# Head turns at half-chunk 21, six output turns one block earlier, and the delta chain respaced, in a two-stage float32 block on one core

## Chip, cores and metric

The kernel runs on one NeuronCore of a Trainium2 chip. The metric is the device time of one execution in microseconds; the profile shows one execution of the same program, instruction by instruction.

## What is computed

Two stages over 256 tokens of width 2048, all in float32. The first holds a gated delta rule with 16 heads, a convolution branch and two gated products; the second holds two layers with memory attention, pooling or block attention, and an output product. The parts that the change touches are these:

```python
qkv = jax.nn.silu(causal_depthwise_conv(qkv, w_conv_qkv[i]))      # per head: q, k, v
o_a = gated_delta_chunked(q, k, v, g_log, beta)                   # 16 heads, chunks of 64
...
mixed = jnp.concatenate([branch * jax.nn.silu(gate_b), mem_o * jax.nn.silu(gate_m)], axis=-1)
y = mixed @ w_out[i]                                              # i = 0, 1
h = layer_norm(DEEPNORM_ALPHA * h + y, ln_g[i], ln_b[i])
```

## The kernel before

**Blocks and half-chunks.** All large products are one long row of blocks. A block is 256 tokens by 512 weight columns, contracted over 2048 channels: 16 chunks of 128 channels, each for two tiles of 128 tokens. A chunk for one tile is a half-chunk (`hs`, 0 to 31 in a block). In each, PE runs three matmuls into a `pair` bank (L460 to L462): the weights are split into a high and a low part (`w_hi`, `w_lo`), and so are the activations (`in_hi`, `in_lo`). The splits are made beside it: ACT copies a raw weight chunk to `w_hi` (L434), DVE subtracts it to `w_lo` (L441), both up to six chunks ahead of PE; `w_hi` and `w_lo` hold eight chunks, so that ACT waits on `chunk_used`, which PE raises after each chunk. SP loads the raw weights.

**Work beside the blocks.** Everything else is hung into the same half-chunks of the four engines by hand: each `..._pe`, `..._act`, `..._dve` function is called with `hs` after PE's three matmuls of that half-chunk, after ACT's piece at even `hs`, and before DVE's piece at odd `hs`. The numbers in `if hs == ...` are therefore the order on each engine, and semaphores connect the engines. All engines run their own list in order.

**Head blocks (0 to 15, their beside work one block later).** Per head: PE turns the projected q, k, v to channel columns at `hs` 3 (L514), DVE and ACT make the four-tap convolution (L544, L607), ACT takes the tanh at 14 (L548), DVE the silu at 16 (L616, `silu_done`), PE turns the result to tokens (L520) and multiplies keys by keys and queries (L525) at 19, ACT copies the tokens to `tok` at 20 (L555) and sums squares at 21 (L564), POOL makes scales of them (L580 to L591), and DVE uses those at `hs` 1 of the next block (L638). The loops over heads run two heads a pass.

**Delta blocks (the four blocks from `BLK_GB`, one group g of four heads each).** A chain passes from PE to ACT or DVE and back through the banks RA, RB and QA: x (PE 2, DVE 3), d (PE 5, DVE 6: `tt`, L899), then for each 128-token tile y (L787), z (L795), v (L800), its copy `vn` on DVE (L907), and the output products. The tile-0 steps stand at 7 to 16 and the tile-1 steps at 17 to 26, where DVE's sum of squares (L925) is the last; POOL turns it into `orn` (L885, L887), and in the next block DVE scales `o_t` with it at `hs` 4 (L934), PE turns that to columns at 8 (L835), ACT and DVE split it (L870, L945). SP waits for steps of this chain before it loads the next group's tiles; the last such load (`tt`, L723) waits for `v_done1`.

**Output blocks (`BLK_OUT0`, `BLK_OUT1`, four blocks each).** Their activations are the gated columns `mo`, turned by PE two channel chunks at a time (a pair or turn g, 0 to 7, four transposes, L1108), copied to `in_hi` by ACT (L1115) and to `in_lo` by DVE (L1121, `turned_lo`). They overwrite the `in_hi`, `in_lo` that the input blocks before still read. Turn 0 stands ahead of the first output block, turns 1 to 7 at its half-chunks 0, 3, 7, 11, 15, 19, 23. The gating of columns 512·n is done by ACT and DVE at `hs` 2 and 5 of the block behind the gate's product (L1680, L1691, L1703, `mixed_ready`); the fourth such one lies in the first output block.

Of the kernel before, what the change touches and what calls it, by code (L numbers as in the profile page):

```python
# [112 lines left out]
def program(nc, t, out, ctx):  # L113
# [393 lines left out]
    def keys_pe(pe, h, hs):  # L507
        if hs == 3:
            pe.wait_ge(psum_free, BLK_A + h + 1)
            reach(pe, s["tok_ready"], h)  # L510
            for c in range(3):
                bank = QB[:, 0:S] if c == 2 else QA[:, c * S:(c + 1) * S]
                for tile in range(TT):
                    mm = pe.transpose(bank[:, tile * P:(tile + 1) * P], proj[:, tile, c * P:(c + 1) * P], ident)  # L514
            mm.then_inc(s["qkv_cols"], 1)
        if hs == 19:
            pe.wait_ge(s["silu_done"], h + 1)
            for tile in range(TT):
                for c in range(3):
                    mm = pe.transpose((QA, QB)[tile][:, c * P:(c + 1) * P], conv[:, c, tile * P:(tile + 1) * P], ident)  # L520
            mm.then_inc(s["qkv_tokens"], 1)
            reach(pe, s["ap_ready"], h)
            for tile in range(TT):
                own = slice(tile * P, (tile + 1) * P)
                mm = pe.matmul(RA[:, tile * S:(tile + 1) * S], conv[:, 1, own], conv[:, 0:2, own], start=True, stop=True)  # L525
            mm.then_inc(s["kk_done"], 1)

    def keys_act(act, h, par, hs):
# [17 lines left out]
        if hs == 14:  # L546
            act.wait_ge(tap_done, SHORT * h + SHORT)
            act.activation(conv_th[:, :, :], conv[:, :, :], ACT.Tanh, scale=0.5).then_inc(s["conv_tanh"], 1)  # L548
        if hs == 20:
            act.wait_ge(s["qkv_tokens"], h + 1)  # L550
            act.wait_ge(s["silu_done"], h + 1)
            act.dma_start(ex_dram[GROUP * (h % GROUP) + h // GROUP, :, EX_KQ:EX_END].rearrange("p (c n) -> p c n", c=2),
                          conv[:, 0:2, P:S]).then_inc(s["kq_stored"], 16)
            reach(act, s["tok_scaled"], h)
            act.activation(tok[:, 0].rearrange("p c n -> p (c n)"), QA[:, 0:3 * P], ACT.Copy)  # L555
            act.activation(tok[:, 1].rearrange("p c n -> p (c n)"), QB[:, 0:3 * P], ACT.Copy)\
               .then_inc(s["tok_ready"], 1)
        if hs == 21:
            act.wait_ge(s["tok_ready"], h + 1)
            reach(act, s["scal_ready"], h)  # L560
            for tile in range(TT):
                for c in range(2):
                    n = 2 * tile + c
                    act.activation(junk[:, n], tok[:, tile, c], ACT.Square, accum_out=ssq[:, n:n + 1])\  # L564
                       .then_inc(s["norms_summed"], 1)
# [195 lines left out]
    def rule_pe(pe, g, hs):  # L761
# [10 lines left out]
        if hs == 5:  # L772
            reach(pe, s["tt_zeroed"], 2 * g)
            for tile in range(TT):
# [3 lines left out]
                mm.then_inc(s["rule_on_pe"], 1)  # L778
        for tile, at in ((0, 7), (1, 17)):
            if hs == at:  # L780
# [16 lines left out]
            if hs == at + 4:  # L797
# [3 lines left out]
                mm.then_inc(s["rule_on_pe"], 1)  # L801
        if hs == 13:
            pe.wait_ge(*step("v_ready0", g))
# [8 lines left out]
            mm.then_inc(s["rule_on_pe"], 1)  # L812
        if hs == 15:
            pe.wait_ge(*step("s1_ready", g))
# [5 lines left out]
            mm.then_inc(s["rule_on_pe"], 1)  # L820
        if hs == 23:
            pe.wait_ge(*step("v_ready1", g))
# [15 lines left out]
    def rule_act(act, g, hs):  # L838
        for tile, at in ((0, 8), (1, 18)):
            if hs == at:  # L840
# [7 lines left out]
        if hs == 14:  # L848
# [3 lines left out]
        if hs == 16:  # L852
            act.wait_ge(*step("qs1_done", g))
# [3 lines left out]
            ins.then_inc(s["rule_on_act"], 1)  # L857
        if hs == 25:
            act.wait_ge(*step("o_ready1", g))
# [29 lines left out]
    def rule_dve(dve, g, hs):  # L889
# [10 lines left out]
        for tile, at in ((0, 12), (1, 22)):  # L900
            if hs == at:
# [5 lines left out]
                dve.tensor_copy(vn[:, :, :], four_of(RA)).then_inc(s["rule_on_dve"], 1)  # L907
        if hs == 14:
# [3 lines left out]
        if hs == 16:  # L912
            dve.wait_ge(*step("ks1_done", g))
# [3 lines left out]
            ins.then_inc(s["rule_on_dve"], 1)  # L917
        if hs == 24:
            dve.wait_ge(*step("o_done1", g))
            dve.wait_ge(*step("oq_ready", g))  # L920
            dve.tensor_tensor(o_t[:, 1], four_of(RB), oq[:, :, :], ALU.add).then_inc(s["rule_on_dve"], 1)
        if hs == 26:
            dve.wait_ge(*step("o_squared", g))
# [831 lines left out]

    OWN_AT = {0: 1, 3: 2, 7: 3, 11: 4, 15: 5, 19: 6, 23: 7}

# [16 lines left out]
    def beside_pe(pe, blk, hs):  # L1774
# [34 lines left out]
        if blk in OWN and hs in OWN_AT:  # L1809
            own_pe(pe, blk, OWN_AT[hs])  # L1810
        if blk in OWN and hs % 4 == 3 and hs < 28:
            pe.wait_ge(s["turned_lo"], OWN[blk][0] + (hs + 1) // 4 + 1)
        pool_pe(pe, blk, hs)
        attention(at, lambda i, h, second: attend_pe(pe, i, h, second))

    def before_pe(pe, blk):
# [17 lines left out]
        if blk in OWN:  # L1834
            own_pe(pe, blk, 0)
            pe.wait_ge(s["turned_lo"], OWN[blk][0] + 1)

# [15 lines left out]
    def beside_act(act, blk, hs):  # L1853
# [94 lines left out]

    def before_act(act, blk):
        if blk in OWN:  # L1950
            own_act(act, blk, 0)

    def tail_act(act):
        for blk in range(BLK_GB, BLK_END):
            before_act(act, blk)
            act_block(act, blk, lambda hs: beside_act(act, blk, hs))
# [5 lines left out]
    def beside_dve(dve, blk, hs):  # L1962
# [457 lines left out]
```

## Time and profile before

| | us |
|---|---|
| median of three runs | 2133.61 (2132.96 to 2133.75) |
| profiled execution | 2134.15 |
| its span, first to last instruction | 2132.1 |
| PE busy | 2100.2 (99%) |
| DVE, ACT, POOL busy | 1474.3 (69%), 1228.0 (58%), 334.6 (16%) |

PE is busy nearly all the time, at a granted clock of 0.998 of full speed. Ends of PE's instructions are modelled, so an idle time of PE in a row is only part of what a wait costs: the distances between starts tell the whole. A regular matmul of a block starts 0.23 us behind the one before it, so that a half-chunk of three takes 0.68 us.

### The profile page before, as it was taken

How to read it: one execution, taken by the hardware profiler on the slowest of the kernel's cores; microseconds unless marked ns; L12 is line 12 of the kernel's file. 1: busy time of each engine (PE TensorE's matmuls, PEld its weight loads, DVE VectorE, ACT ScalarE, POOL GpSimd, SP SyncE). 2: the span in 40 equal slices, each digit the busy share in tenths (PEclk: the TensorE clock that was granted, in tenths of full speed). 3: DMA queues.
4: the chain of work that ended last, by engine and by line, in shares of the span. 5: the costliest groups of instructions: out<-in, count | busy, mean ns of one | idle time of the engine just before them, and what ended most of it. 6: DMA issues, size and time to landing. Idle time of an engine off the chain costs nothing.

```text
span 2132.1 us, 28652 instructions
## 1 busy us (share of the span) xinstructions
PE 2100.2 (99%) x9841; PEld 1733.5 (81%) x9841; DVE 1474.3 (69%) x2676; ACT 1228.0 (58%) x2359; POOL 334.6 (16%) x468
## 2 busy tenths in 40 slices
PE   7999999999999999999999999999999999999998
PEld 6888888888888888888888877887888888888886
DVE  6777777788999977569665655643666745456666
ACT  6666666677777764457555544543554555555543
POOL 1111111156665641010000000000000000000000
PEclk9999999999999999999999999999999999999999
DMA  8777766789877866576777665655665555644462
GB/s 248 231 210 207 201 196 192 202 223 266 228 208 211 233 209 212 191 263 210 260 265 251 224 209 168 212 178 163 233 221 197 182 180 195 197 158 139 158 217 99
DMA packets 434689, 439.68 MB, mean 206 GB/s; under 512 B 27728, under 2 KB 306384, under 8 KB 432144
## 3 DMA queue, kind: packets, MB, share of 16 engines
q1 hardware_dynamic: 412752, 381.76, 58.1%
q0 software_dynamic: 7600, 35.79, 5.0%
q10 hardware_dynamic: 14224, 20.71, 2.7%
q8 instruction: 61, 1.00, 0.2%
q14 instruction: 52, 0.43, 0.1%
HBM read 410.92 MB, written 27.28 MB: 206 GB/s over the span
## 4 chain that ended last, share of the span: by engine, by line
PE 81%; DVE 14%; issue 2%; ACT 2%; DMA 0%; POOL 0%; DVEq 0%; SPq 0%; POOLq 0%; ACTq 0%
PE pair L460 24%; PE pair L462 24%; PE pair L461 24%; DVE w_lo L441 5%; DVE conv L607 2%; DVE QB L1058 2%; ACT conv L544 1%; PE QA L1489 1%; PE RA L1505 1%; PE RA L525 1%; DVE conv L616 1%; DVE ap L659 1%; DMA raw<-in_w_in_dram 0%; PE QB L1574 0%; PE QA L520 0%
## 5 line engine op out<-in xcount | busy, mean ns | idle before, releaser
L441 DVE TENSOR_TENSOR w_lo<-raw,w_hi 128x512 fp32r<-128x512 f32 x1368 | 920.8, 692 | 401.1 <-ACT w_hi L434 399.2
L434 ACT ACTIVATE w_hi<-raw 128x512 fp32r<-128x512 f32 x1368 | 826.9, 625 | 450.4 <-PE pair L462 445.0
L460 PE MATMUL pair<-w_hi,in_hi 128*128 128x512 f32 x2336 | 932.9, 399 | 3.9 <-DVE in_lo L1121 2.8
L462 PE MATMUL pair<-w_hi,in_lo 128*128 128x512 f32 x2336 | 911.1, 390 | 0.0
L461 PE MATMUL pair<-w_lo,in_hi 128*128 128x512 f32 x2336 | 909.8, 389 | 0.0
L462 PEld LDWEIGHTS pair<-w_hi,in_lo 128*128 128x128 f32 x2336 | 438.4, 188 | 93.4
L460 PEld LDWEIGHTS pair<-w_hi,in_hi 128*128 128x128 f32 x2336 | 439.0, 188 | 92.5 <-DVE in_lo L1121 3.3
L461 PEld LDWEIGHTS pair<-w_lo,in_hi 128*128 128x128 f32 x2336 | 439.2, 188 | 87.9 <-issue 1.0
L1027 POOL TENSOR_TENSOR acc_p<-acc_p,tap 128x256 f32<-128x256 f32 x160 | 184.2, 1151 | 38.7 <-ACT tap L1001 25.3
L1001 ACT ACTIVATE tap<-upad,cwl 128x256 f32<-128x256 f32 x192 | 96.7, 507 | 51.9 <-POOL acc_p L1027 50.9
L1058 DVE SCALAR_TENSOR_TENSOR QB<-upad,cwl,QB 128x256 f32<-128x256 f32 x272 | 119.5, 478 | 0.0
L607 DVE SCALAR_TENSOR_TENSOR conv<-conv_in,cw,conv 128x256 f32<-128x256 f32 x144 | 61.1, 479 | 7.4 <-ACT conv L544 7.4
L2106 POOL DMA_DIRECT2D ln_vec_a<-in_ln_g_dram x1 | 0.5, 531 | 350.7 <-DVE mo L1703 350.7
L580 POOL TENSOR_TENSOR an<-ssq,pool_eps 128x4 f32<-128x4 f32 x16 | 3.2, 201 | 333.5 <-ACT junk L564 333.5
L460 PE MATMUL pair<-w_hi,mem_hi 128*128 128x512 f32 x128 | 51.9, 406 | 0.0
L460 PE MATMUL pair<-w_hi,oa_hi 128*128 128x512 f32 x128 | 50.9, 398 | 0.0
L460 PE MATMUL pair<-w_hi,ub_hi 128*128 128x512 f32 x128 | 50.2, 392 | 0.0
L462 PE MATMUL pair<-w_hi,mem_lo 128*128 128x512 f32 x128 | 50.1, 391 | 0.0
L461 PE MATMUL pair<-w_lo,mem_hi 128*128 128x512 f32 x128 | 50.0, 390 | 0.0
L462 PE MATMUL pair<-w_hi,oa_lo 128*128 128x512 f32 x128 | 49.9, 390 | 0.0
L461 PE MATMUL pair<-w_lo,oa_hi 128*128 128x512 f32 x128 | 49.9, 390 | 0.0
L462 PE MATMUL pair<-w_hi,ub_lo 128*128 128x512 f32 x128 | 49.9, 390 | 0.0
(394 smaller groups left out, 1806.8 us busy)
## 6 DMA issues: line engine op xcount, KB each, us to landing
raw<-in_w_in_dram SPq DMA_DIRECT2D x512, 256.0 KB, 4.0
raw<-in_w_in_dram SPq DMA_DIRECT2D x80, 1024.0 KB, 5.2
raw<-in_w_out_dram SPq DMA_DIRECT2D x48, 1024.0 KB, 5.0
raw<-in_w_kv_shared_dram SPq DMA_DIRECT2D x24, 1024.0 KB, 5.1
raw<-in_w_br_a_dram SPq DMA_DIRECT2D x16, 1024.0 KB, 6.4
raw<-in_w_br_b_dram SPq DMA_DIRECT2D x16, 1024.0 KB, 6.8
raw<-in_w_mem_kv_dram SPq DMA_DIRECT2D x16, 1024.0 KB, 5.0
raw<-in_w_ple_gate_dram SPq DMA_DIRECT2D x16, 1024.0 KB, 5.0
```

The costliest lines, as they stand in the source:

```text
L434: act.activation(piece(blk, q)[0], raw[:, u, q % UK], ACT.Copy).then_inc(hi_ready[u], 1)
L441: dve.tensor_tensor(lo, raw[:, u, q % UK], hi.bitcast(F32), ALU.subtract).then_inc(lo_ready[u], 1)
L460: pe.matmul(o, xh, wh, start=(q == 0), stop=False)
L461: pe.matmul(o, xh, wl, start=False, stop=False)
L462: mm = pe.matmul(o, xl, wh, start=False, stop=(q == KC - 1))
L525: mm = pe.matmul(RA[:, tile * S:(tile + 1) * S], conv[:, 1, own], conv[:, 0:2, own], start=True, stop=True)
L544: ins = act.activation(conv[:, c], conv_in[:, c, 0:S], ACT.Copy, scale=cw[:, 0, c:c + 1])
L607: ins = dve.scalar_tensor_tensor(conv[:, c], conv_in[:, c, k:k + S], cw[:, k, c:c + 1], conv[:, c], ALU.mult, ALU.add)
L616: dve.scalar_tensor_tensor(conv[:, :, :], conv_th[:, :, :], 1.0, conv[:, :, :], ALU.add, ALU.mult)\
L1001: act.activation(tap[:, n % 2], upad[:, par, k:k + S], ACT.Copy, scale=cwl[:, k:k + 1])\
L1027: pool.tensor_tensor(acc_p[:, :], tap[:, 0] if n == 1 else acc_p[:, :], tap[:, n % 2], ALU.add)\
L1058: dve.scalar_tensor_tensor(a, src, cwl[:, k:k + 1], a, ALU.mult, ALU.add).then_inc(long_tap[k % 2], 1)
```

## The change

No instruction is added and none is taken away; places in the order move. Three parts:

- Heads: PE's turn to tokens goes from `hs` 19 to 21, with it ACT's copy from 20 to 22 and its squares from 21 to 23.
- Delta chain: tile 0's y, z, v from 7, 9, 11 to 8, 10, 12, `vn` from 12 to 13, the products behind it from 13 and 15 to 15 and 17, tile 1's from 17, 19, 21 to 20, 22, 24, `vn` from 22 to 25, the rest from 23 to 26 to 26 to 30.
- Output turns: 0 to 5 go to half-chunks 12, 14, 17, 20, 24, 28 of the last input block, where ACT waits for the old columns to have been used (`chunk_used`); 6 and 7 stand at 8 and 10 of the first output block. PE waits once for six `turned_lo` ahead of that block, and for all eight at its `hs` 23.

```diff
 def keys_pe(pe, h, hs):
-        if hs == 19:
+        if hs == 21:
             pe.wait_ge(s["silu_done"], h + 1)
...
 def rule_pe(pe, g, hs):
-        for tile, at in ((0, 7), (1, 17)):
+        for tile, at in ((0, 8), (1, 20)):
             if hs == at:
                 pe.wait_ge(*step("t64_ready1", g))
...
-        if hs == 13:
+        if hs == 15:
             pe.wait_ge(*step("v_ready0", g))
...
 def rule_dve(dve, g, hs):
-        if hs == 26:
+        if hs == 30:
             dve.wait_ge(*step("o_squared", g))
...
-    OWN_AT = {0: 1, 3: 2, 7: 3, 11: 4, 15: 5, 19: 6, 23: 7}
+    OWN_AHEAD = {12: 0, 14: 1, 17: 2, 20: 3, 24: 4, 28: 5}
+    OWN_AT = {8: 6, 10: 7}
...
+    def own_ahead_pe(pe, blk, g):
+        if g == 0:
+            heads = MEM_HEADS if blk == BLK_OUT0 else len(ATTEND)
+            pe.wait_ge(s["att_ready"], heads)
+            pe.wait_ge(s["probT_ready"], heads)
+            pe.wait_ge(s["scores_masked"], heads)
+        own_pe(pe, blk, g)
+
+    def own_ahead_act(act, blk, g):
+        act.wait_ge(chunk_used, (KC - 1) * (blk - 1) + 2 * g + 2)
+        own_act(act, blk, g)
...
-        if blk in OWN and hs % 4 == 3 and hs < 28:
-            pe.wait_ge(s["turned_lo"], OWN[blk][0] + (hs + 1) // 4 + 1)
+        if blk in OWN and hs == 23:
+            pe.wait_ge(s["turned_lo"], OWN[blk][0] + 8)
+        if blk + 1 in OWN and hs in OWN_AHEAD:
+            own_ahead_pe(pe, blk + 1, OWN_AHEAD[hs])
...
         if blk in OWN:
-            own_pe(pe, blk, 0)
-            pe.wait_ge(s["turned_lo"], OWN[blk][0] + 1)
+            pe.wait_ge(s["turned_lo"], OWN[blk][0] + 6)
```

PE in a head block, at the turn to tokens (`silu_done` is DVE's silu, `lo_ready2` a chunk of `w_lo`):

```order
 L461 MATMUL pair<-w_lo,in_hi 128x512
 L462 MATMUL pair<-w_hi,in_lo 128x512
+L460 MATMUL pair<-w_hi,in_hi 128x512 [waits lo_ready2]
+L461 MATMUL pair<-w_lo,in_hi 128x512
+L462 MATMUL pair<-w_hi,in_lo 128x512
+L460 MATMUL pair<-w_hi,in_hi 128x512
+L461 MATMUL pair<-w_lo,in_hi 128x512
+L462 MATMUL pair<-w_hi,in_lo 128x512
 L520 MATMUL QA<-const,conv 128x128 [waits silu_done]
 L520 MATMUL QA<-const,conv 128x128 x2
```

Two half-chunks of the block's own matmuls now stand ahead of the waiting transposes.

PE at the start of the first output block, before:

```order
L462 MATMUL pair<-w_hi,in_lo 128x512
L1108 MATMUL QA<-const,mo 128x128 [waits turned_lo,mixed_ready]
L1108 MATMUL QA<-const,mo 128x128 x3
L460 MATMUL pair<-w_hi,in_hi 128x512 [waits lo_ready0,psum_free,turned_lo]
L461 MATMUL pair<-w_lo,in_hi 128x512
L462 MATMUL pair<-w_hi,in_lo 128x512
L1108 MATMUL QB<-const,mo 128x128 [waits turned_lo,mixed_ready]
L1108 MATMUL QB<-const,mo 128x128 x3
```

and in the changed program, from the last turn of the input block on (`turned_lo` is DVE's low part of the turned columns):

```order
L1108 MATMUL QB<-const,mo 128x128 [waits turned_lo,mixed_ready]
L1108 MATMUL QB<-const,mo 128x128 x3
L460 MATMUL pair<-w_hi,in_hi 128x512
L461 MATMUL pair<-w_lo,in_hi 128x512
L462 MATMUL pair<-w_hi,in_lo 128x512
L460 MATMUL pair<-w_hi,in_hi 128x512 [waits lo_ready3]
L461 MATMUL pair<-w_lo,in_hi 128x512
L462 MATMUL pair<-w_hi,in_lo 128x512
L460 MATMUL pair<-w_hi,in_hi 128x512
L461 MATMUL pair<-w_lo,in_hi 128x512
L462 MATMUL pair<-w_hi,in_lo 128x512
L460 MATMUL pair<-w_hi,in_hi 128x512 [waits lo_ready0,psum_free,turned_lo]
```

Turn 0 stood between the blocks and was waited for at once; now nothing stands between them, and the wait for `turned_lo` has three half-chunks behind turn 5.

PE in the second delta block, half-chunks 6 to 8, before (`rule_on_dve` is the chain's `tt`, `og_ready` DVE's scaled `o_t`):

```order
L460 MATMUL pair<-w_hi,in_hi 128x512
L461 MATMUL pair<-w_lo,in_hi 128x512
L462 MATMUL pair<-w_hi,in_lo 128x512
L787 MATMUL RA<-vbk_113,tt_112 128x128 [waits vbk_loaded,rule_on_dve]
L787 MATMUL RA<-vbk_113,tt_112 128x128 x3
L460 MATMUL pair<-w_hi,in_hi 128x512 [waits lo_ready1]
L461 MATMUL pair<-w_lo,in_hi 128x512
L462 MATMUL pair<-w_hi,in_lo 128x512
L835 MATMUL QA<-const,o_t 128x128 [waits u_ready,og_ready]
L835 MATMUL QA<-const,o_t 128x128 x3
L835 MATMUL QB<-const,o_t 128x128 x4
```

and in the changed program, from the same half-chunk on:

```order
L460 MATMUL pair<-w_hi,in_hi 128x512
L461 MATMUL pair<-w_lo,in_hi 128x512
L462 MATMUL pair<-w_hi,in_lo 128x512
L460 MATMUL pair<-w_hi,in_hi 128x512 [waits lo_ready1]
L461 MATMUL pair<-w_lo,in_hi 128x512
L462 MATMUL pair<-w_hi,in_lo 128x512
L787 MATMUL RA<-vbk_113,tt_112 128x128 [waits vbk_loaded,rule_on_dve]
L787 MATMUL RA<-vbk_113,tt_112 128x128 x3
L835 MATMUL QA<-const,o_t 128x128 [waits u_ready,og_ready]
L835 MATMUL QA<-const,o_t 128x128 x3
L835 MATMUL QB<-const,o_t 128x128 x4
```

The chain's step L787 goes behind one more half-chunk and stands directly ahead of the turns L835. On ACT, in the same block, the split of those turned columns (L870) stood behind the chain's copy L847 and now stands ahead of it.

## Rows read from the trace of the kernel before

**Rows 1.** The page, busy time of each engine.
```profile
PE 2100.2 (99%) x9841; PEld 1733.5 (81%) x9841; DVE 1474.3 (69%) x2676; ACT 1228.0 (58%) x2359; POOL 334.6 (16%) x468
```
**Rows 2.** Waits of PE, PEld, ACT: line <- releaser: us in total, times, longest.
```profile
PE QA L520 <- DVE conv L616: 3.5, 15, 0.2
PE pair L460 <- DVE in_lo L1121: 2.8, 2, 1.4
...
PEld QA L520 <- DVE conv L616: 9.9, 15, 0.7
...
PEld RA L787 <- DVE tt L899: 2.0, 3, 1.1
...
PEld RB L805 <- DVE vn L907: 1.8, 3, 0.7
...
ACT w_hi L434 <- PE pair L462: 445.0, 603, 4.6
```
**Rows 3.** Timeline of PE at a head's turn: start us, us, instruction [idle <-releaser].
```profile
228.81 0.39 PE L462 MATMUL pair<-w_hi,in_lo 128*128 128x512 f32 x1
229.43 0.55 PE L520 MATMUL QA<-const,conv 128*128 128x128 f32 x3 [0.23 <-DVE conv L616]
229.81 0.49 PE L520 MATMUL QB<-const,conv 128*128 128x128 f32 x3
```
**Rows 4.** Timeline of PE at a turn of the same block that doesn't wait.
```profile
217.24 0.39 PE L462 MATMUL pair<-w_hi,in_lo 128*128 128x512 f32 x1
217.47 0.60 PE L514 MATMUL QA<-const,proj 128*128 128x128 f32 x4
217.91 0.38 PE L514 MATMUL QB<-const,proj 128*128 128x128 f32 x2
```
**Rows 5.** Timeline of DVE in the same head, from the first tap to the silu.
```profile
220.72 1.28 DVE L607 SCALAR_TENSOR_TENSOR conv<-conv_in,cw,conv 128x256 f32<-128x256 f32 x3 [0.44 <-ACT conv L544]
...
228.42 0.95 DVE L616 SCALAR_TENSOR_TENSOR conv<-conv_th,conv 128x768 f32<-128x768 f32 x1
```
**Rows 6.** Timelines of ACT, POOL and DVE from a head's turn into the next block.
```profile
215.53 0.68 ACT L534 ACTIVATE proj<-pair,small 128x512 f32<-128x512 f32 x1
...
211.25 0.19 POOL L591 TENSOR_TENSOR scal<-scal,hst 128x2 f32<-128x2 f32 x1
...
213.50 0.48 DVE L638 TENSOR_SCALAR ex<-tok,scal 128x128 f32<-128x128 f32 x2
```
**Rows 7.** Timeline of PE at the start of the first output block.
```profile
1569.08 0.60 PE L1108 MATMUL QA<-const,mo 128*128 128x128 f32 x4
1571.09 0.50 PE L460 MATMUL pair<-w_hi,in_hi 128*128 128x512 f32 x1 [1.41 <-DVE in_lo L1121]
...
1571.89 0.60 PE L1108 MATMUL QB<-const,mo 128*128 128x128 f32 x4
1572.25 0.48 PE L460 MATMUL pair<-w_hi,in_hi 128*128 128x512 f32 x1
```
**Rows 8.** Timelines of PE and DVE at the start of the last input block.
```profile
1547.31 0.39 PE L460 MATMUL pair<-w_hi,in_hi 128*128 128x512 f32 x1
...
1550.54 1.23 DVE L1703 TENSOR_TENSOR mo<-mo,stage 128x1024 f32<-128x1024 f32 x1
```
**Rows 9.** Timelines of PE and DVE in the second delta block, the waiting step.
```profile
814.74 0.40 PE L462 MATMUL pair<-w_hi,in_lo 128*128 128x512 f32 x1
815.77 1.16 PE L787 MATMUL RA<-vbk,tt 128*128 128x128 f32 x8 [0.64 <-DVE tt L899]
...
815.03 0.68 DVE L899 TENSOR_TENSOR tt<-RB,tt 128x512 f32<-128x512 f32 x1
```
**Rows 10.** SP's `tt` loads there, landing of all loads of L723, PE's next need.
```profile
835.96 2.15 SPq L723 DMA_DIRECT2D tt<-inverse_blocks  x4
...
DMA to landing us min/median/max: 2.0/4.2/9.8
...
845.53 1.05 PE L770 MATMUL RA<-t,ap 128*128 128x128 f32 x8
```

More of the change, by code:

```diff
@@ L548, in keys_act @@
             act.activation(conv_th[:, :, :], conv[:, :, :], ACT.Tanh, scale=0.5).then_inc(s["conv_tanh"], 1)
-        if hs == 20:
+        if hs == 22:
             act.wait_ge(s["qkv_tokens"], h + 1)
@@ L557, in keys_act @@
                .then_inc(s["tok_ready"], 1)
-        if hs == 21:
+        if hs == 23:
             act.wait_ge(s["tok_ready"], h + 1)
@@ L812, in rule_pe @@
             mm.then_inc(s["rule_on_pe"], 1)
-        if hs == 15:
+        if hs == 17:
             pe.wait_ge(*step("s1_ready", g))
@@ L820, in rule_pe @@
             mm.then_inc(s["rule_on_pe"], 1)
-        if hs == 23:
+        if hs == 26:
             pe.wait_ge(*step("v_ready1", g))
@@ L838, in rule_act @@
     def rule_act(act, g, hs):
-        for tile, at in ((0, 8), (1, 18)):
+        for tile, at in ((0, 9), (1, 21)):
             if hs == at:
@@ L847, in rule_act @@
                 act.activation(zneg[64:P].rearrange("p h n -> p (h n)"), RB[64:P, :], ACT.Copy, scale=-1.0).then_inc(s["rule_on_act"], 1)
-        if hs == 14:
+        if hs == 16:
             act.wait_ge(*step("s1_done", g))
@@ L851, in rule_act @@
             act.activation(s1[:, :, :].rearrange("p h n -> p (h n)"), RB[:, :], ACT.Copy).then_inc(s["rule_on_act"], 1)
-        if hs == 16:
+        if hs == 18:
             act.wait_ge(*step("qs1_done", g))
@@ L857, in rule_act @@
             ins.then_inc(s["rule_on_act"], 1)
-        if hs == 25:
+        if hs == 28:
             act.wait_ge(*step("o_ready1", g))
@@ L899, in rule_dve @@
                 dve.tensor_tensor(tt4[:, tile], four_of((RA, RB)[tile]), tt4[:, tile], ALU.add).then_inc(s["rule_on_dve"], 1)
-        for tile, at in ((0, 12), (1, 22)):
+        for tile, at in ((0, 13), (1, 25)):
             if hs == at:
@@ L907, in rule_dve @@
                 dve.tensor_copy(vn[:, :, :], four_of(RA)).then_inc(s["rule_on_dve"], 1)
-        if hs == 14:
+        if hs == 16:
             dve.wait_ge(*step("o_done0", g))
@@ L911, in rule_dve @@
             dve.tensor_copy(o_t[:, 0], four_of(QA)).then_inc(s["rule_on_dve"], 1)
-        if hs == 16:
+        if hs == 18:
             dve.wait_ge(*step("ks1_done", g))
@@ L917, in rule_dve @@
             ins.then_inc(s["rule_on_dve"], 1)
-        if hs == 24:
+        if hs == 27:
             dve.wait_ge(*step("o_done1", g))
@@ L1930, in beside_act @@
             own_act(act, blk, OWN_AT[hs])
+        if blk + 1 in OWN and hs in OWN_AHEAD:
+            own_ahead_act(act, blk + 1, OWN_AHEAD[hs])
         attention(at, lambda i, h, second: attend_act(act, i, h, second))
@@ L2040, in beside_dve @@
             own_dve(dve, blk, OWN_AT[hs])
+        if blk + 1 in OWN and hs in OWN_AHEAD:
+            own_dve(dve, blk + 1, OWN_AHEAD[hs])
         if hs == 0 and (BLK_OUT0 <= done < BLK_OUT0 + 3 or BLK_OUT1 <= done):
@@ L2061, in ple_dve @@
                .then_inc(s["mo_scaled"], 1)
-    def before_dve(dve, blk):
-        if blk in OWN:
-            own_dve(dve, blk, 0)
     def tail_dve(dve):
         for blk in range(BLK_GB, BLK_END):
-            before_dve(dve, blk)
             dve_block(dve, blk, lambda hs: beside_dve(dve, blk, hs))
```

4 lines of the change are left out of this document (removed).

## Prediction

> **What bounds the kernel.** I read the page first: PE is busy for 99% of the span, DVE for 69%, ACT for 58% [rows 1]. So PE's own list sets the time, and since the change adds and removes no instruction, only PE's waits can pay. The list of waits shows which there are [rows 2]: fifteen waits of the heads' turn L520 for DVE's silu, two of an output block's first matmul for `in_lo`, and, best seen on PE's weight loads (PEld), three of the chain's L787 for `tt` and three of L805 for `vn`. Idle time is only a part of what such a wait costs, so I then took timelines of PE around one wait of each kind and measured from start to start.
>
> **Heads' turns, hs 19 to 21.** Ahead of L520 the last matmul starts at 228.81 and the first transpose at 229.43: 0.62 us [rows 3]. The turn L514, which waits for nothing, starts 0.23 us behind its matmul [rows 4]. That is 0.39 us lost. The three transposes after the wait take 0.38 us (229.43 to 229.81), where four without one take 0.44 (217.47 to 217.91), so three 0.33: 0.05 more. 0.44 us a head, 15 heads: **6.6 us**.
>
> Would the wait be gone? DVE ends the silu at 229.37 [rows 5], just ahead of PE's 229.43. Two half-chunks of three matmuls at 0.23 us bring PE there 1.36 us later than it could before, and the wait was 0.39, so PE comes 0.97 us after the silu. The silu doesn't move with it: nothing from the first tap on waits for the turn, and the pieces of ACT and DVE in between are held by PE's chunks as before.
>
> What is late instead: ACT's copy and squares, POOL's scales, and DVE's use of them at hs 1 of the next block. POOL ends at 211.44, DVE starts at 213.50 [rows 6]: 2.06 us to spare. The turn comes 0.92 us later in its block (1.36 less 0.44) and the next block begins 0.44 us sooner, so 0.70 us are left. ACT's drain of the next product ends at 216.21 [rows 6], 1.26 us ahead of the turn L514 at 217.47 [rows 4] that reads it. The DMA of old queries and keys that ACT issues at hs 20 moves with the copy to 22; `conv` is written again only at hs 5 of the next block. I take nothing for these.
>
> **Output turns.** The first turn starts at 1569.08 and the block's first matmul at 1571.09, 2.01 us, where a turn inside the block takes 0.36 (1571.89 to 1572.25) [rows 7]. The difference, 1.65 us, is lost ahead of each of the two output blocks: the waits of rows 2 are two, with 1.4 us of idle each. **3.3 us.** The eight turns themselves cost PE the same in any block. Two new places to wait:
> - Turn 5 is at hs 28 and the output block waits for its `turned_lo`. From its start PE has 0.36 us of transposes and three half-chunks, 2.04 us, together 2.40, and 2.01 are needed [rows 7]. 0.4 us to spare; at worst, one more 128x512 step of DVE in the way (0.68 us as in rows 9), 0.3 us a block.
> - Turn 6 moves from hs 19 to hs 8 of the output block and needs the fourth gating. One block earlier the third gating ends at 1551.77, 4.46 us behind that block's first matmul at 1547.31 [rows 8]. PE reaches its turn at hs 8 after nine half-chunks, 6.1 us. 1.6 us to spare, as ACT and DVE no longer begin the block with turns.
>
> In the input block ACT and DVE get six turns, in a block where ACT waits for PE's chunks anyway (0.74 us a time, rows 2), and the attention that shares the banks has ended. Nothing.
>
> **Delta chain.** At its worst place the last matmul starts at 814.74 and L787 at 815.77 [rows 9]: 1.03 us against 0.23, 0.80 lost and a little for the restart. For all six I scale from the heads, where PEld's idle is 9.9/15 = 0.66 us for a loss of 0.44, the idle less 0.22. L787: 2.0 - 3 x 0.22 = 1.3 us; L805: 1.8 - 0.66 = 1.1; 2.4 together [rows 2]. One half-chunk more (0.68 us) ahead of L787 covers the two shorter waits (0.9 us of PEld idle for both) and all but 0.1 of the long one: PE arrives at 815.65 for a `tt` that DVE ends at 815.71 [rows 9]. L805 gets a half-chunk more behind the step that feeds `vn`. I take **2.3**, and 1.0 as the lower end, if DVE, busy without a break ahead of `tt` there, slips with PE.
>
> What is late instead: the last sum of squares goes from hs 26 to 30, and DVE's use of POOL's result stays at hs 4 of the next block. SP's loads of `tt`, which wait for PE's step `v`, go back by three half-chunks, 2.04 us. They are issued from 835.96 to 838.11, land 4.2 us after issue in the median, and PE needs them at 845.53 [rows 10]: 838.11 + 2.04 + 4.2 = 844.35, 1.2 us to spare. The weight load behind them in SP's queue waits for DVE's piece at hs 27 and so isn't held up. Nothing.
>
> **Sum.** 6.6 + 3.3 + 2.3 = 12.2 us. Against the profiled execution of 2134.15 (span 2132.1 and 2.05 around it) that is 2121.95; the median of the runs lies 0.54 lower than that execution, so **2121.4 us**, 0.57% faster. The three terms stand one after the other on PE's list, so they add.
>
> **Two rules of a page.** The Trainium skill ("Perfetto Trace Analysis", Tensor Engine Instruction) says that the end of a PE instruction in a profile is an estimate, while its start is observed. The trace agrees: 128x512 matmuls listed at 0.39 us start 0.23 apart. By it the idle rows understate a wait, which speaks for the start distances and against the third rival.
> The same page (Identifying Performance Opportunities, "Consistent bubbles") says that one gap repeated over a stretch can mean too little buffer space. By that rule fifteen equal gaps would not go away with a later place; the first rival is that case.
>
> **Rivals.**
> - The heads' wait comes back: the silu depends on space that PE frees, and is as late at hs 21 as at 19. Then 12.2 - 6.6 = 5.6 us remain: 2128.0. For it: the gap is the same in every head. Against it: DVE is busy from 220.72 to 229.37 and started on ACT's first tap [rows 5], which hangs on PE's hs 3 at 217.47 [rows 4]. That chain has a fixed length of 11.9 us, and PE's way gets 1.36 us longer.
> - The output blocks wait again, at turn 5 or at the gating for turn 6: up to 3.3 us given back, 2124.7. The 0.4 or the 1.6 us above would have to be used up.
> - The rest of each start distance is no wait and stays. Then PE's idle counts: 3.5 + 2.8, and for the chain 3.8 of PEld's idle by the heads' ratio 3.5/9.9, 1.3: 7.6 us in all, 2126.0. Against it: L514 has the same neighbours and not that distance [rows 4].
> - **Slower**: ACT's copy and squares, 0.92 us later in a block that ends 0.44 sooner, push ACT's drain past the turn L514 that reads it. The margin is 1.26 [rows 4, 6], the shift 1.36, so even with no recovery PE waits 0.1 us. If ACT also loses a piece and its wait for PE (0.74 us, rows 2), or more, PE waits w in each of 16 heads: 2121.4 + 16 w. From w = 0.77 us that is slower than before, and w = 1.1 gives 2139.0. Against it: ACT has such a wait for PE at nearly each chunk, and makes up for the shift in two of them.
> - The `tt` loads land late. With 9.8 us, the longest in rows 10, PE waits 4.4 us in each of three blocks, 13 us, and nothing is left: 2134.6.
>
> **Chances and range.** Forecast 0.78; heads' wait back 0.08; output blocks 0.04; idle rows 0.04; `tt` late 0.03; slower 0.03. The forecast's own range is 2119.8 (restart costs of 0.1 us at the chain's six places, and 1 us between runs) to 2123.3 (chain 1.0, 0.3 at each output block). With the output and idle cases beside it, 2119.8 to 2126.0 leaves 0.14 out, and holds 8 in 10 with some error of my own. A measurement here can tell 0.2%, 4.3 us, from no change. Below 2129.3 are all cases but the last two: faster 0.93, no change 0.04, slower 0.03.
>
> **What would show it.** In the profile after: no wait of L520 for L616, and 0.23 us from matmul to L520 in every head; no wait of L460 for L1121, and 0.23 us across the start of both output blocks; L787 and L805 with one short wait at most. The prediction is wrong if a wait of PE for DVE, ACT or a DMA is new at L514, L770, L1108 or at the new place of L520.

## The result, and the profile after

The changed kernel takes 2120.56 us in the median of four runs (2119.98 to 2120.67), beside 2133.40 (2132.96 to 2133.75) of the kernel before measured on the same chip. The ratio is 0.9937, with a 95% interval of 0.9926 to 0.9949: 12.84 us less, where 12.2 us were forecast (the forecast time was 2121.4 us). The profiled execution took 2119.98, its span 2118.2.

The page of after, busy time of each engine, answers to [rows 1]: PE has the same 9841 instructions.

```profile
PE 2094.6 (99%) x9841; PEld 1735.4 (82%) x9841; DVE 1472.7 (70%) x2676; ACT 1226.7 (58%) x2359; POOL 336.3 (16%) x468
```

PE's whole list of waits after (line <- releaser: us in total, times, longest) answers to [rows 2].

```profile
PE pair L1197 <- DVE in_lo L1137: 10.9, 1, 10.9
PE QA L971 <- DVE z2b L1040: 0.7, 3, 0.3
PE QA L1108 <- DVE xr L1615: 0.6, 1, 0.6
PE QB L1369 <- DVE sqb L1418: 0.4, 1, 0.4
PE QA L1226 <- DVE sgl L1321: 0.3, 1, 0.3
PE pair L460 <- DVE w_lo L441: 0.3, 1, 0.3
PE QA L1223 <- DVE sgl L1316: 0.2, 1, 0.2
```

The lines of L520, of L460 for L1121, of L787 and of L805 are gone, on PE and on PEld, and no line is new. What is left is in stages that the change doesn't touch; the longest, L1197, is PE's first instruction, which starts 10.9 us into the program.

A head's turn after, in timelines of PE (start us, us, instruction), DVE, and PE at the turn L514 of the same block, answers to [rows 3 to 5].

```profile
226.74 0.39 PE L462 MATMUL pair<-w_hi,in_lo 128*128 128x512 f32 x1
226.97 0.49 PE L520 MATMUL QA<-const,conv 128*128 128x128 f32 x3
227.30 0.49 PE L520 MATMUL QB<-const,conv 128*128 128x128 f32 x3
...
225.00 0.95 DVE L616 SCALAR_TENSOR_TENSOR conv<-conv_th,conv 128x768 f32<-128x768 f32 x1
...
214.05 0.60 PE L514 MATMUL QA<-const,proj 128*128 128x128 f32 x4
```

L520 now starts 0.23 us behind its matmul, not 0.62, and three transposes take 0.33, not 0.38. The silu ends at 225.95, 1.02 us ahead of L520, and 11.90 us behind this block's L514 (214.05), as before (217.47 to 229.37).

The start of the first output block after, PE and DVE, answers to [rows 7] and, for the fourth gating, to [rows 8].

```profile
1558.85 0.60 PE L1108 MATMUL QB<-const,mo 128*128 128x128 f32 x4
1559.20 0.48 PE L460 MATMUL pair<-w_hi,in_hi 128*128 128x512 f32 x1
...
1561.14 0.40 PE L462 MATMUL pair<-w_hi,in_lo 128*128 128x512 f32 x1
1561.37 0.39 PE L460 MATMUL pair<-w_hi,in_hi 128*128 128x512 f32 x1
...
1567.50 0.60 PE L1108 MATMUL RA<-const,mo 128*128 128x128 f32 x4
...
1560.17 0.69 DVE L1121 SCALAR_TENSOR_TENSOR in_lo<-QB,in_hi 128x512 fp32r<-128x512 f32 x1 [1.30 <-ACT in_hi L1115]
...
1564.60 1.23 DVE L1703 TENSOR_TENSOR mo<-mo,stage 128x1024 f32<-128x1024 f32 x1
```

The output block begins at 1561.37, 0.23 us behind the matmul before it. Turn 5 (1558.85) has its last piece at 1560.86, 0.51 us ahead. The gating ends at 1565.83, turn 6 starts at 1567.50.

The second delta block after, PE and DVE, answers to [rows 9]; here PE starts L787 0.22 us behind its matmul and L805 0.23.

```profile
807.88 0.39 PE L462 MATMUL pair<-w_hi,in_lo 128*128 128x512 f32 x1
808.10 1.05 PE L787 MATMUL RA<-vbk,tt 128*128 128x128 f32 x8
...
807.05 0.68 DVE L899 TENSOR_TENSOR tt<-RB,tt 128x512 f32<-128x512 f32 x1
...
816.23 0.39 PE L462 MATMUL pair<-w_hi,in_lo 128*128 128x512 f32 x1
816.46 0.72 PE L805 MATMUL RB<-vn,vbk 128*128 128x128 f32 x5
```

**The sum from both traces.** With the start distances of every place, each less the undisturbed 0.23 us (or 0.11 between transposes), the kernel before loses 5.91 + 0.86 = 6.77 us at L520, 3.31 at the two output blocks, and 1.55 + 1.35 = 2.90 at L787 and L805. That is 12.98 us, and 0 at all of them after. The median fell by 12.84. The spans of the two profiled executions differ by 13.9 us, and 0.8 of that lies ahead of the first head's turn L514, at a wait at the program's start (L460 for `w_lo`, 1.1 us before and 0.3 after), which differs from execution to execution and which the change doesn't touch (last section).

### The profile page after: what moved, and what is told of

Its sections match the earlier page's. It is cut to its first block, busy times and chain, and to the rows that moved or that the text cites. A ratio compares the mean times of both kernels' runs of the same rounds, so it can differ in the third digit from the quotient of the medians.

```text
span 2118.2 us, 28654 instructions
## 1 busy us (share of the span) xinstructions
PE 2094.6 (99%) x9841; PEld 1735.4 (82%) x9841; DVE 1472.7 (70%) x2676; ACT 1226.7 (58%) x2359; POOL 336.3 (16%) x468
## 4 chain that ended last, share of the span: by engine, by line
PE 89%; DVE 8%; issue 1%; ACT 1%; DMA 1%; POOL 1%; DVEq 0%; ACTq 0%; POOLq 0%
PE pair L460 26%; PE pair L462 26%; PE pair L461 26%; DVE w_lo L441 3%; DVE QB L1058 2%; PE QA L1489 1%; PE RA L1505 1%; PE RA L525 1%; POOL acc_p L1027 0%; PE QB L1574 0%; PE RA L1731 0%; PE RB L1731 0%; DMA x_cols<-in_x_columns_dram 0%; PE pair L481 0%; PE pair L482 0%
## 5 line engine op out<-in xcount | busy, mean ns | idle before, releaser
L441 DVE TENSOR_TENSOR w_lo<-raw,w_hi 128x512 fp32r<-128x512 f32 x1368 | 919.6, 693 | 392.9 <-ACT w_hi L434 391.0
L460 PE MATMUL pair<-w_hi,in_hi 128*128 128x512 f32 x2336 | 932.8, 399 | 0.3 <-DVE w_lo L441 0.3
L460 PEld LDWEIGHTS pair<-w_hi,in_hi 128*128 128x128 f32 x2336 | 439.0, 188 | 88.5 <-DVE w_lo L441 1.1
L460 PE MATMUL pair<-w_hi,mem_hi 128*128 128x512 f32 x128 | 51.9, 406 | 0.0
L460 PE MATMUL pair<-w_hi,oa_hi 128*128 128x512 f32 x128 | 50.9, 398 | 0.0
L460 PE MATMUL pair<-w_hi,ub_hi 128*128 128x512 f32 x128 | 50.2, 392 | 0.0
```

The lines of the kernel that those rows point to most:

```text
L441: dve.tensor_tensor(lo, raw[:, u, q % UK], hi.bitcast(F32), ALU.subtract).then_inc(lo_ready[u], 1)
L460: pe.matmul(o, xh, wh, start=(q == 0), stop=False)
```

## Experiments

The kernels ran in three sets, each on a chip of its own with the kernel before beside it: 2133.93 us in the first, 2133.69 in the second and 2133.74 in the third. Gains in the medians are taken against the kernel before of the same set. Intervals of ratios are of 95%, against the kernel before.

### The three parts, each alone

Heads alone (`heads_only`), on the kernel before:

```diff
-        if hs == 19:
+        if hs == 21:
             pe.wait_ge(s["silu_done"], h + 1)
...
-        if hs == 20:
+        if hs == 22:
             act.wait_ge(s["qkv_tokens"], h + 1)
...
-        if hs == 21:
+        if hs == 23:
             act.wait_ge(s["tok_ready"], h + 1)
```

> The kernel before with the heads' turns alone moved (19 to 21, and their two ACT steps by two). Theory of the prediction: what a wait costs is the distance from the end of the turn's last matmul before it to the start of L520, here 0.44 us in each of 15 heads, so 6.6 us less than before, about 2126.8. Rival: only the idle time that the PE rows name is worth something (some 0.23 us a head), so 3.5 us less, about 2130. Second rival: the span follows the longest engine and not the wait, so nothing.

Measured: 2127.28 us (2126.98 to 2128.53), ratio 0.9970 (0.9959 to 0.9981): 6.65 us less. The rival of idle rows (2130) falls, and so does that of no gain.

Output turns alone (`own_only`), the core of the edit:

```diff
-    OWN_AT = {0: 1, 3: 2, 7: 3, 11: 4, 15: 5, 19: 6, 23: 7}
+    OWN_AHEAD = {12: 0, 14: 1, 17: 2, 20: 3, 24: 4, 28: 5}
+    OWN_AT = {8: 6, 10: 7}
...
-            own_pe(pe, blk, 0)
-            pe.wait_ge(s["turned_lo"], OWN[blk][0] + 1)
+            pe.wait_ge(s["turned_lo"], OWN[blk][0] + 6)
```

> The kernel before with the six gated pairs turned in the block ahead, and the last two at half-chunks 8 and 10 of the output block. Theory: 1.65 us in each of the two output blocks, 3.3 us less than before, about 2130.1. Rival by idle rows alone: 2.8 less. Rival that the turns in the input block cost PE time of their own: less than 3.3 by about 0.3 us for each block.

Measured: 2130.25 us (2129.45 to 2131.80), ratio 0.9984 (0.9975 to 0.9993): 3.68 us less, for 3.3 expected. Its trace shows that the turns cost nothing more in the input block: each starts 0.23 or 0.24 us behind its matmul and takes 0.35 or 0.36, as inside an output block before. Between 3.3 and the idle rows' 2.8 the median alone doesn't decide, since the interval holds both; the starts (3.31) are what speaks for the first.

The chain alone (`chain_only`), the core of the edit:

```diff
-        for tile, at in ((0, 7), (1, 17)):
+        for tile, at in ((0, 8), (1, 20)):
...
-        if hs == 13:
+        if hs == 15:
             pe.wait_ge(*step("v_ready0", g))
...
-        for tile, at in ((0, 12), (1, 22)):
+        for tile, at in ((0, 13), (1, 25)):
             if hs == at:
                 dve.wait_ge(*step(f"v_done{tile}", g))
```

> The kernel before with the delta chain's steps alone at half-chunks 8 to 30. Theory: the waits of L787 and L805 go, whose start distances beyond an undisturbed step add up to 2.9 us, of which the prediction took 2.3 and kept 0.1 as left over; about 2130.8. Rival by idle rows: 1.3 less, about 2132.1. If this alone gives nothing, the three parts don't add up and the gain of the whole sits elsewhere.

Measured: 2130.51 us (2130.30 to 2131.59), ratio 0.9986 (0.9977 to 0.9995): 3.42 us less. Its trace has no wait of L787 or L805. The idle rows' 1.3 us falls (it would give 2132.6); the start distances' 2.9 stands, 0.5 below what was measured. The three gains add up to 13.75 us, where the whole gave 12.84, 0.9 less. All three are taken against the same median of the kernel before, so that an error in it counts three times, and that median differs by up to 0.5 us between the sets (2133.40 to 2133.93). So the parts add to within 1 us, and these medians can't show more; by the starts in the traces the three terms add to 12.98.

### What the wait at L520 is made of

Here L520 is put nearer and further away in the kernel after. (Where the expectation says "ACT's silu", the silu is DVE's, L616.) First `heads18`:

```diff
-        if hs == 21:
+        if hs == 18:
             pe.wait_ge(s["silu_done"], h + 1)
...
-        if hs == 22:
+        if hs == 20:
             act.wait_ge(s["qkv_tokens"], h + 1)
...
-        if hs == 23:
+        if hs == 21:
             act.wait_ge(s["tok_ready"], h + 1)
```

> The kernel after with the heads' turns on PE at half-chunk 18 and ACT's steps at 20 and 21. Theory of the prediction (ACT's silu ends at a time fixed by the head's earlier steps, so PE loses every step by which it comes sooner): at 19 PE lost 0.44 us, at 18 it comes 0.68 us earlier and loses 1.12 us, in 15 heads 16.8 us more than the kernel after, about 2137.4. Rival (the loss is a fixed hand-over between PE and ACT wherever the turn stands): 0.44 us a head, about 2127.2.

Measured: 2137.66 us (2137.18 to 2138.38), ratio 1.0019 (1.0009 to 1.0029), against 2137.4 by the theory and 2127.2 by the rival. The kernel is slower than before. Its timelines of PE and DVE at the same head:

```profile
231.75 0.39 PE L462 MATMUL pair<-w_hi,in_lo 128*128 128x512 f32 x1
233.07 0.55 PE L520 MATMUL QA<-const,conv 128*128 128x128 f32 x3 [0.93 <-DVE conv L616]
233.46 0.49 PE L520 MATMUL QB<-const,conv 128*128 128x128 f32 x3
...
232.07 0.95 DVE L616 SCALAR_TENSOR_TENSOR conv<-conv_th,conv 128x768 f32<-128x768 f32 x1
```

PE starts L520 1.32 us behind its matmul, 1.09 more than undisturbed, and loses 0.06 among the transposes: 1.15 us a head, 17.2 in fifteen. The median rose by 17.1. The row itself says 0.93. At 19 the loss was 0.44, so one half-chunk (0.68 us) costs 0.71: the silu ends 11.91 us behind L514 (221.11 to 233.02), the same time as before, and PE pays each step by which it is early.

`heads20` has 20, 21, 22 in the same three places.

> The kernel after with the heads' turns at 20, ACT's steps at 21 and 22. Theory: silu ends 1.02 us ahead of L520 at 21, so 0.34 us ahead at 20: no wait, same as the kernel after within 0.2 us, about 2120.6. Rival (a fixed hand-over, which 21 escapes by an accident of order): 0.44 us a head, about 2127.2.

Measured: 2120.38 us (2120.22 to 2122.24), ratio 0.9940 (0.9923 to 0.9957). No wait of L520. PE and DVE at the same head:

```profile
226.16 0.39 PE L462 MATMUL pair<-w_hi,in_lo 128*128 128x512 f32 x1
226.38 0.49 PE L520 MATMUL QA<-const,conv 128*128 128x128 f32 x3
...
225.10 0.94 DVE L616 SCALAR_TENSOR_TENSOR conv<-conv_th,conv 128x768 f32<-128x768 f32 x1
```

The silu ends at 226.04, 0.34 us ahead, and 11.90 us behind L514. Half-chunk 20 gives the whole gain; 21 gives reserve.

`heads27` has 27, 28, 29, which tries the slower rival.

> The kernel after with the heads' turns at 27, ACT's steps at 28 and 29: six half-chunks, 4.1 us, later than in the kernel after. It tries the slower rival of the prediction. In the kernel after ACT's scaled copy of tile 1 (L534) ends 1.26 us ahead of L514 and DVE's L638 0.64 us ahead of what needs it. Theory: both margins are set by the steps that follow the turn at fixed places, and the next head's conv waits for them; with 4.1 us taken from 1.26 a wait of L514 would be 2.8 us a head, some 42 us, unless L514 of the next head stands far enough behind half-chunk 29. By the order of the program L514 comes in the next head at half-chunk 14 to 18, so I count on no wait at L514, and on DVE's part of the conv being about 1.4 us late without PE waiting for it: about 2120.6. Rival: a wait that comes to PE costs 15 times its size.

Measured: 2120.68 us (2120.41 to 2121.15), ratio 0.9939 (0.9923 to 0.9956), and no new wait of PE. ACT, POOL, DVE and PE of `heads27` from the turn into the next block:

```profile
211.64 0.69 ACT L533 ACTIVATE proj<-pair,small 128x512 f32<-128x512 f32 x1
212.23 0.68 ACT L534 ACTIVATE proj<-pair,small 128x512 f32<-128x512 f32 x1
...
212.53 0.20 POOL L591 TENSOR_TENSOR scal<-scal,hst 128x2 f32<-128x2 f32 x1
...
212.94 0.48 DVE L638 TENSOR_SCALAR ex<-tok,scal 128x128 f32<-128x128 f32 x2 [1.08 <-POOL scal L591]
```

and of the kernel after, the same drain:

```profile
211.52 0.69 ACT L533 ACTIVATE proj<-pair,small 128x512 f32<-128x512 f32 x1 [0.73 <-PE pair L462]
212.11 0.68 ACT L534 ACTIVATE proj<-pair,small 128x512 f32<-128x512 f32 x1
```

In the kernel after ACT idles 0.73 us for PE ahead of its drain (L533). In `heads27` that idle is used up, and the drain still ends 1.26 us ahead of L514 (212.91, L514 at 214.17). The drain is no step of the change; it only stands behind ACT's moved steps, and even six half-chunks don't reach it. POOL's scales end at 212.73, and DVE waits 1.08 us for them at L638 (1.4 expected), which PE doesn't notice. The expected time was right for a reason that was wrong: L514 does not stand at half-chunk 14 to 18 of the next block but at 3, as before. What keeps the margin is that the drain doesn't move.

### Which part of the chain's edit removes L805's wait

`chain_plus1` is the kernel after with the late steps closer together:

```diff
-        for tile, at in ((0, 8), (1, 20)):
+        for tile, at in ((0, 8), (1, 18)):
...
-        if hs == 15:
+        if hs == 14:
             pe.wait_ge(*step("v_ready0", g))
...
-        for tile, at in ((0, 13), (1, 25)):
+        for tile, at in ((0, 13), (1, 23)):
```

> The kernel after with the chain's steps closer together: each of the late steps one half-chunk later than in the kernel before (18 for the second y, z and v on PE, 14 for v of the first tile, 16 and 24 for the rest) and not two and three. Theory A (the extra half-chunk is what lets DVE's step come in time for L805): L805 waits again, some 0.4 us in each of three groups, 1.2 us more than the kernel after, about 2121.8. Theory B (what counts is that ACT's oa_hi stands ahead of zneg there, so DVE's oa_lo and vn follow without idling): same as the kernel after, about 2120.6, with no wait of L805 over 0.1 us.

Measured: 2120.63 us (2120.48 to 2121.25), ratio 0.9940 (0.9926 to 0.9953). L805 waits nowhere. So the third half-chunk between v (PE 12) and L805 (14 here, 15 in the kernel after) is not needed, and theory B is left, but this run keeps the new order on ACT and the later start of the chain together. The next run parts them: `oa_first` is the kernel before with one number changed. (`oa_hi`, the first part of the turned columns, is ACT's L870; `oa_lo` is DVE's L945.)

```diff
     def oa_act(act, g, hs):
-        if hs == 10:
+        if hs == 9:
```

> The kernel before with one thing changed: ACT's oa_act (L863, the copies oa_hi L870) stands at half-chunk 9 and not 10, so that it comes ahead of zneg L847 instead of behind it. No step of the delta chain moves. Theory (the order on ACT causes L805's wait: zneg waits 1.5 us for PE with oa_hi behind it, DVE idles ahead of oa_lo L945, and vn L907 comes late): vn comes at least 1 us earlier, the waits of L805 go, 1.0 us less, about 2132.5, while L787's waits stay with 1.2 us. Rival (the chain needs the extra half-chunks on PE): L805 waits as before, same time as the kernel before within 0.3 us.

Measured: 2132.32 us (2131.76 to 2133.16), ratio 0.9992 (0.9983 to 1.0001): 1.4 us less for 1.0 expected, which by itself is at the edge of what can be told from nothing. By the starts L805 loses 1.35 us in the kernel before and nothing here. The trace decides. First the kernel before, ACT, DVE and PE in the second delta block:

```profile
820.12 0.59 ACT L847 ACTIVATE zneg<-RB 64x512 f32<-64x512 f32 x1 [1.53 <-PE RB L795]
820.74 0.60 ACT L870 ACTIVATE oa_hi<-QA 128x512 fp32r<-128x512 f32 x1
...
821.37 0.69 DVE L945 TENSOR_TENSOR oa_lo<-QA,oa_hi 128x512 fp32r<-128x512 f32 x1 [4.45 <-ACT oa_hi L870]
...
823.17 0.68 DVE L907 COPY vn<-RA 128x512 f32<-128x512 f32 x1
...
823.91 0.82 PE L805 MATMUL RB<-vn,vbk 128*128 128x128 f32 x5 [0.16 <-DVE vn L907]
```

then `oa_first`, the same steps:

```profile
817.34 0.60 ACT L870 ACTIVATE oa_hi<-QA 128x512 fp32r<-128x512 f32 x1 [0.53 <-PE QA L835]
...
819.37 0.59 ACT L847 ACTIVATE zneg<-RB 64x512 f32<-64x512 f32 x1 [0.42 <-PE RB L795]
...
817.97 0.69 DVE L945 TENSOR_TENSOR oa_lo<-QA,oa_hi 128x512 fp32r<-128x512 f32 x1 [1.80 <-ACT oa_hi L870]
...
821.63 0.69 DVE L907 COPY vn<-RA 128x512 f32<-128x512 f32 x1 [1.77 <-PE RA L800]
...
822.58 0.39 PE L462 MATMUL pair<-w_hi,in_lo 128*128 128x512 f32 x1
822.81 0.94 PE L805 MATMUL RB<-vn,vbk 128*128 128x128 f32 x7
...
815.02 0.82 PE L787 MATMUL RA<-vbk,tt 128*128 128x128 f32 x5 [0.65 <-DVE tt L899]
```

Before, oa_hi stands on ACT behind zneg, and zneg waits 1.53 us for PE. DVE therefore idles 4.45 us ahead of oa_lo, then works through its queue, and `vn` follows late and without a break. With oa_hi ahead of zneg, DVE is through with its queue early and waits only for PE in front of `vn` (1.77 us). `vn` ends at 822.32, 0.49 us ahead of L805, where it ended at 823.85 before, 0.26 us after PE had come to L805 (0.23 us behind the matmul at 823.36). Against PE's matmul ahead of L805, `vn` comes 0.75 us earlier, less than the 1 us that was expected, and enough. No step of the chain has moved, L805's wait is gone in all three blocks, and L787's is still there (0.65). **The cause of L805's wait is the order on ACT.** The change makes the same swap, as it moves zneg from half-chunk 10 to 11, behind oa_hi, and the swap alone is enough. Whether a half-chunk more ahead of L805 would also have been enough, with oa_hi still behind zneg, no run tried. L787's wait is of the other kind: it stays with the swap, and goes where PE comes to it one half-chunk later (`chain_only`, `chain_plus1`, the kernel after).

### How near the new places of the output turns are to their limits

`own_tight` is the kernel after with

```diff
-    OWN_AHEAD = {12: 0, 14: 1, 17: 2, 20: 3, 24: 4, 28: 5}
-    OWN_AT = {8: 6, 10: 7}
+    OWN_AHEAD = {12: 0, 14: 1, 17: 2, 20: 3, 24: 4, 30: 5}
+    OWN_AT = {5: 6, 10: 7}
```

> The kernel after with turn 5 at half-chunk 30 and not 28 of the block ahead, and turn 6 at 5 and not 8 of the output block. Theory by margins: turn 5's copy on DVE takes 2.01 us from the turn's start to its end, and the output block starts 1.04 us after half-chunk 30's turn, so its first matmul waits about 0.97 us in each of two blocks; the gating ends 4.46 us into the block and PE comes to turn 6 after 4.1 us, so 0.4 to 0.5 us more in each. Together some 2.8 us, about 2123.4. Rival (the copy's slack is hidden because the first matmuls read the earlier pairs): only turn 6's 0.9, about 2121.5.

Measured: 2123.21 us (2122.93 to 2123.49), ratio 0.9950 (0.9933 to 0.9967): 2.65 us more than after, 2.8 expected. PE and DVE of it:

```profile
1561.84 0.40 PE L462 MATMUL pair<-w_hi,in_lo 128*128 128x512 f32 x1
1563.01 0.51 PE L460 MATMUL pair<-w_hi,in_hi 128*128 128x512 f32 x1 [0.77 <-DVE in_lo L1121]
...
1567.01 0.39 PE L462 MATMUL pair<-w_hi,in_lo 128*128 128x512 f32 x1
1567.34 0.66 PE L1108 MATMUL RA<-const,mo 128*128 128x128 f32 x4
...
1566.06 1.23 DVE L1703 TENSOR_TENSOR mo<-mo,stage 128x1024 f32<-128x1024 f32 x1
```

The start distance across the block is 1.17 us, 0.94 lost, for 0.97 expected. The rival, that the first matmuls only read early pairs and don't wait, falls: the wait stands ahead of the whole block. The second half of my sum was wrong in its split: for the 0.4 to 0.5 us expected at turn 6 the trace shows a third. It loses 0.10 us (0.33 less 0.23) and 0.06 among its transposes. The block began late by the wait at turn 5, the gating did not move with it by as much (it ends 4.28 us behind the block's start and not 4.46), and PE reached turn 6 at 4.23. The first wait paid for most of the second. From the rows 0.94 + 0.11 (the second matmul after the wait starts 0.34 behind it) + 0.16 = 1.2 us a block, 2.4 in all.

### A try at a faster one

The waits that are left after the change have DVE as releaser. `late_turns` moves two of their kinds later:

```diff
     def group_pe(pe, j, par, hs):
-        if hs == 9:
+        if hs == 10:
             pe.wait_ge(s["glu_ready"], j + 1)
...
-        if blk in X_TURNS and hs >= 12 and hs % 2 == 0 and hs < 28:
-            g = (hs - 12) // 2
+        if blk in X_TURNS and hs >= 14 and hs % 2 == 0 and hs < 30:
+            g = (hs - 14) // 2
```

(the second edit on PE, ACT and DVE alike), with the kernel after once more beside it.

> A try to beat the kernel after: that kernel with PE's turns of glu and z2b (L971) at half-chunk 10 and not 9, and the turns of xr (L1804, L1927, L2033) at half-chunks 14 to 28 and not 12 to 26. Expected from start distances beyond an undisturbed step in the kernel after: L971 loses 0.49, 0.31 and 0.37 us in three blocks, L1108 behind xr loses 0.72 us once; 1.9 us less than the kernel after, about 2118.7. Rival: DVE's taps behind L971 start 0.7 us later in each block and the wait comes back at the next block's start, so same as the kernel after or more.

> The kernel after once more, on the same chip as the two others: 2120.6 within 0.5 us by every theory. It gives the run beside it its zero.

Measured: `late_turns` 2119.84 us (2119.39 to 2120.22), ratio 0.9934 (0.9920 to 0.9948); the kernel after 2121.03 (2120.31 to 2121.54), ratio 0.9940 (0.9927 to 0.9954). 1.2 us less, where 1.9 were expected; the ranges of the runs don't touch, but the intervals overlap. Counted from the first head's turn L514 (46.25 us and 45.81), the two profiled spans differ by 0.8 us, about what the wait for xr makes. Its list of waits has this row of L971, and none of L1108:

```profile
PE QA L971 <- DVE z2b L1040: 0.7, 3, 0.3
```

The wait for xr (0.72 us by starts) is gone, that of L971 is as large as before. One half-chunk later on PE gave nothing there. Busy time in a stretch of 23 us of the kernel after, where the wait is, points to why (us, then the busy us of PE, PEld, DVE, ACT and POOL, the granted clock, DMA share and GB/s):

```profile
592.00:615.00 23.00, 22.84 (x103) 18.64 (x102) 22.86 (x48) 17.41 (x34) 14.41 (x14) 1.00 0.77 206
```

DVE is busy for 22.86 of 23 us, as long as PE. From one z2b (L1040) to the next it needs 22.69 us there (590.07 to 612.76), and in `late_turns` 22.71 (591.27 to 613.98), while PE's group takes 22.25 where it doesn't wait (434.31 to 456.56). When PE comes later, `u` reaches DVE later, its taps start later and what follows slips by the same amount: counted from PE's matmul at the old place (612.68, here 613.21), z2b starts 0.69 us later, which is the half-chunk. For L971 the expectation's rival held. A busy share alone doesn't make the wait, for DVE is as busy from 638 to 661 us (22.86 of 23), where PE doesn't wait. And whether z2b slips because DVE is full or because its taps hang on the step that was moved, this run doesn't part.

## Why the prediction was right, point by point

- **Heads' turns, 6.6 us.** 6.77 us by the starts in both traces, 6.65 by the run alone. The margin of 0.97 us behind the silu is 1.02. The silu did not move with PE's turn: it ends 11.90 or 11.91 us behind L514 with the turn at 18, 19, 20 and 21.
- **Scales and drain.** DVE's L638 starts at 210.08 and POOL's last scale ends at 209.44: 0.64 us, for 0.70 forecast. ACT's drain is 1.26 us ahead of L514 as before. The slower rival set the shift of 1.36 against that margin, with ACT's idle time in between as the doubt; the idle time decides, and the margin is not touched. `heads27` puts the turn 4.1 us later still and PE doesn't wait.
- **Output turns, 3.3 us.** 3.31 us by the starts, 3.68 by the run alone. Turn 5 has 0.51 us to spare for 0.4 forecast, turn 6 comes 6.13 us into the block for a gating at 4.46: the two figures were 6.1 and 4.46. `own_tight` shows the waits come back once both margins are used up.
- **Chain, 2.3 us.** The term that was mis-sized: 2.90 us by the starts, 3.42 by the run alone. I scaled PE's loss from PEld's idle with the heads' difference of 0.22 us. That was right for L787 at its worst place (1.03 less 0.23 is 0.80, and 1.1 less 0.22 is 0.88) but left out the step's own matmuls behind the wait, 0.1 us further apart at each of six places (0.63 in all), which I had only put into the range. And the left-over of 0.1 us at L787 did not come: in the second delta block DVE ends `tt` at 807.73, 0.37 us ahead of PE. DVE began its step L894 1.55 us behind PE's L770 (801.95 against 800.40), where it was 1.98 before (809.93 against 807.95). The traces of the other runs place it: the distance is 1.98 or 1.99 us in `heads_only`, `own_only` and `oa_first`, 1.73 in `chain_plus1` and 1.54 in `chain_only`. So it is the later places of the chain's own steps that shorten DVE's queue ahead of the next group, and without that PE would still have come 0.06 us too early. Which of these steps does it, no run parts.
- **And its mechanism at L805.** The prediction said that L805 "gets a half-chunk more behind the step that feeds `vn`". The size held, the reason was not the one needed: `oa_first` removes the same wait without any half-chunk, and `chain_plus1` has none more between v and L805. The swap on ACT was in the listing of the change ahead of the prediction, and I didn't use it.
- **`tt` loads.** SP now issues them from 829.07 to 831.61, and PE's L770 starts at 836.60 without a wait, 4.99 us behind the last issue, where it was 7.42. I had forecast 2.04 us less distance and it became 2.43 less. No wait of L770 is new, so that the rival of late loads falls.
- **The two rules.** Start distances: 12.98 us by them, 12.84 measured, where PE's idle rows gave 7.6. The Trainium skill ("Perfetto Trace Analysis", Tensor Engine Instruction) says that the profiler estimates a PE instruction's end, while its start is when the instruction begins to fetch its data. On the ends this case agrees (matmuls listed at 0.39 us start 0.23 apart), and `heads18` shows again what it means for a wait, with 1.15 us lost under a row that says 0.93. The same page of the Trainium skill (Identifying Performance Opportunities, "Consistent bubbles") says that a gap that repeats can mean too little buffer space. That is not the cause here: the fifteen equal gaps were 1.15, 0.44 and 0 us with the turn at 18, 19 and 20, in the same buffers.

## What to carry to other kernels

Cost a wait of the bounding engine by the distance between the starts around it, the instructions behind it included, and not by its idle row. Before you move a waiting step later, ask what made the releaser late: a chain of fixed length is outrun by a later place, down to a few tenths of a us; a result that stands behind another wait in its engine's queue is freed by swapping two instructions there; and a result of an engine that is busy all the time, whose work hangs on the step that you move, slips along with you (one try, `late_turns`). Margins worked out from the starts in one trace held to 0.1 us at the heads and the output turns, so the first place without a wait can be computed there. In the delta chain, where the moved steps change DVE's queue as well, two margins were 0.4 us off. And of two waits in a row the first pays for part of the second.

## What the runs showed beyond that

- The wait at the program's start (L460 for L441, first block, no kernel changes anything there) is between 0.2 us (the kernel after, third set) and 1.5 us in the profiled executions, and not in the list at all for `chain_only`. PE's first instruction (L1197) starts between 10.0 and 10.9 us, and the first head's turn L514 between 45.5 and 46.7. So two spans can differ by 1.2 us without a cause in the change, and terms below that are read from places, not from spans. This is the row of `chain_plus1`, whose span is 2118.9, beside 0.3 and 2118.2 of the kernel after; their medians are 2120.63 and 2120.56.

```profile
PE pair L460 <- DVE w_lo L441: 1.5, 1, 1.5
```
- `heads_only` has one wait of L971 more than every other kernel: 0.9 us in the fifth group of the stage behind the heads (at 524.95).

```profile
PE QA L971 <- DVE z2b L1040: 1.7, 4, 0.9
```

  It isn't there in the kernel after, which has the same edit among its three. Its trace shows what came late, a load of the gate's bias that DVE waits for 4 us earlier:

```profile
520.56 0.42 DVE L1034 TENSOR_TENSOR bproj<-bproj,bg 128x256 f32<-128x256 f32 x1 [1.38 <-DMA bg<-in_b_gate_dram]
```

  That load landed 6.5 us after its issue, where the longest of the same loads in the kernel after took 4.9. It is seen in one profiled execution, the slowest of the seven runs; why the load took longer stays open.
